# Long runs of contraction steps in the first two tiles of each phase, with later norm sums behind layer 2 and an early table load, in an eight-core streaming encoder trunk

## The chip, the cores and the metric

The kernel runs as one program on the 8 NeuronCores of one Trainium2 chip (two dies, cores 0 to 3 and 4 to 7). Each core works on its own tokens; nothing is exchanged between cores. The metric is the device time in microseconds of the slowest core. Engines are named as in the profile: PE is TensorE (PEld its weight loads), DVE is VectorE, ACT is ScalarE, POOL is GpSimd, SP is SyncE; SPq and POOLq are the queues on which DMAs are issued.

## What is computed

Four layers, all of the same outer form, on activations of width 1024 (inner width 2048):

```
h   = rms_norm(x) * (1 + scale) + shift          # scale, shift, gate from a conditioning vector
br  = h @ w_in                                   # 2, 3 or 4 branches of 2048 channels, one of them z
y   = mixer(branches)                            # 0: gated MLP over positions, 1: short conv,
                                                 # 2: conv of width 31 + layer norm, 3: pooling
x   = x + gate * ((y * silu(z)) @ w_out)         # w_out: 2048 -> 1024
```

Layer 0 applies GELU to the branches u and v, layer 2 a sigmoid to the branch ag (`glu = a * sigmoid(ag)`); a final RMS norm follows layer 3. Each core has some 2100 token columns, held in SBUF with channels on the partitions.

## The kernel before

**Groups and phases.** A core's columns are two groups, g = 0 (1074 columns with the halo, 1056 in the later layers) and g = 1 (1024 prompt columns and 32 of the decode request). Every layer runs, for g = 0 and then for g = 1, an *in phase* (`h @ w_in` and the mixer, result in `ysT`, 16 chunks of 128 channels) and an *out phase* (`ysT @ w_out`, 8 output tiles d = 0 to 7, added to x). That makes 8 in phases and 8 out phases. Below, (2,0) is layer 2, group 0.

**A tile** is 128 output channels by one group's columns, three PSUM banks wide: per contraction step (128 input channels) PE does three matmuls of 358 or 352 columns. An in tile has 8 steps (24 matmuls), an out tile 16 (48 matmuls). `tile_mm` (L456) issues them, so that nearly all matmuls of the profile have line 461. Only two such *slots* exist (`next_slot`, L282): slots take turns, and the first matmul into a slot waits until ACT or DVE has emptied it (the eviction of the tile before the last). The banks 6 and 7 beside them take norm sums and the adaLN product.

**Order of work.** `Sched` (L46) records instructions engine by engine in program order and puts a semaphore wait only where the data asks for one. Engines are in-order, so the order in the program is the order on each engine. Weights come through a ring of 8 tiles of SBUF (`pump`, L297): whenever PE is done with a tile, `release` (L315) issues the next load on the POOL queue, in a fixed order.

**Start of an in phase.** h is produced at the end of the out phase before it by DVE (`apply`, L441: `scale` L430, then `modulate` L437), 8 chunks, the last one only after the eviction of out tile 7. So the first in tile is issued in single contraction steps, each with its own wait for its chunk of h: with `fine=True` in `inproj` (L466) for layers 1 to 3. In layer 0, `inproj_first` (L477) alternates between the first two tiles at every step:

```python
for kc in range(8):
    for ci in range(2):
        tile_mm(sls[ci], nc_ // 3, [(w[:, kc, ...], hT[:, kc, ho:ho + nc_])], [wkey, "h.%d" % kc], kc == 0, kc == 7)
```

**The out phase** (`out_phase`, L502) first calls the hooks of index -1, then alternates tile 0 and tile 1 at every one of the 16 steps (L520 to L522), since the last chunks of `ysT` come late, and then goes on with tiles 2 to 7 one by one. DVE adds every tile to x (L536; for g = 1 a second, short instruction, L542, corrects the decode columns). After each tile d come the hooks of index d, which make the *other* group's next norm (`norm_hooks`, L1205):

```python
hooks = {-1: [lambda d=d: sq(d) for d in range(8)],
         1: [lambda d=d: stats(d) for d in range(8)] + [rstd],
         2: [bc]}
for d, which in ((3, (0,)), (4, (1, 2)), (5, (3, 4)), (6, (5, 6)), (7, (7,))):
    hooks[d] = [lambda i=i: apply(i) for i in which]
```

`sq` is 8 squares on ACT (L400), `stats` 24 short matmuls that sum them (L407), `rstd` is an add and a reciprocal on DVE (L413, L414) and a square root on ACT (L415, with an activation table load), `bc` a broadcast by PE into the next slot (L423) with its copy on ACT (L427).

**Layer 2** ends its in phase with a pipeline over the 16 chunks: `center` (L1007), `norm` (L1013 on DVE, then a SiLU on ACT, L1015) and `product` (L1022 on DVE).

## Time and profile before

| | |
|---|---|
| three timed runs | 2281.91, 2282.03, 2287.24 us; median 2282.03 us |
| profiled execution: span of the slowest core (core 5) | 2280.8 us |
| spans of the 8 cores in it | 2267.7 to 2280.8 us |
| mean granted PE clock, core 5 | 0.978 |
| median of die 0, of die 1 | 2272.2 us, 2274.4 us |
| PE busy on core 5 | 2135.5 us (94% of the span) |

The span runs from the first to the last instruction of one profiled execution; that execution's own time outside it is not listed, and the span lies 1.2 us below the median of the timed runs. A busy time of a group of matmuls is from the start of the first to the modelled end of the last: three matmuls alone show 0.61 us, of which some 0.15 us is the last one's way through the engine and not time that the next one must wait. So distances between starts are the better measure, and the idle time in brackets is a little low. In the waits, "PE ps L461 <- ACT ysT L649" is idle time of PE before a matmul that was ended by ACT's instruction of line 649.

### The profile page before, as it was taken

What the parts mean: (1) busy time and instruction counts of PE and PEld (TensorE: products, weight loads), DVE (VectorE), ACT (ScalarE), POOL (GpSimd) and SP (SyncE); (2) the same over time, 40 slices, a digit from 0 to 9 for tenths busy, and PEclk for the clock granted to TensorE, in tenths of its full rate; (3) what the DMA queues carried; (4) which work ended last, traced back from release to release, by engine and by line L of the source; (5) the groups of instructions that cost most, each with busy time, mean ns of one, the idle gap of its engine ahead of it and who ended that gap; (6) DMA issues with size and microseconds to landing.
All of it is one profiled execution on the core that took longest, in us unless ns stands there. A gap on an engine that the chain in (4) does not pass through costs nothing.

```text
span 2280.8 us, 41000 instructions; the slowest of 8 cores (2267.7 to 2280.8 us)
## 1 busy us (share of the span) xinstructions
PE 2135.5 (94%) x15851; PEld 1324.3 (58%) x15851; DVE 1045.9 (46%) x1482; ACT 670.2 (29%) x854; POOL 321.1 (14%) x593
## 2 busy tenths in 40 slices
PE   4999999998999999999999997999989999999996
PEld 1644655445666666666666664566655566666653
DVE  3444150442455454655545322753316566455535
ACT  3254303543011112111121334703446322303331
POOL 1012001111000100001002441104430000000000
PEclk9999999999999999999999998999999999999998
DMA  9905848057344644346445994538974444444423
GB/s 204 203 24 89 134 74 134 16 91 141 65 67 69 105 69 81 65 75 111 75 75 112 192 195 97 104 64 192 200 173 70 81 68 73 73 71 69 81 45 150
DMA packets 90637, 232.43 MB, mean 102 GB/s; under 512 B 16400, under 2 KB 41616, under 8 KB 90288
## 3 DMA queue, kind: packets, MB, share of 16 engines
q0 software_dynamic: 53264, 181.82, 45.3%
q1 hardware_dynamic: 37184, 48.00, 7.9%
q8 instruction: 130, 2.13, 0.4%
q14 instruction: 59, 0.48, 0.1%
HBM read 339.51 MB, written 9.55 MB: 153 GB/s over the span
## 4 chain that ended last, share of the span: by engine, by line
PE 82%; DVE 6%; DMA 5%; issue 2%; ACT 2%; SPq 2%; DVEq 0%; POOL 0%; ACTq 0%; POOLq 0%
PE ps L461 73%; PE ps L684 5%; DMA ring<-w_in_a 2%; SPq L130 2%; DMA ring<-w_ada 1%; PE ps L937 1%; DMA tmp<-tmp 1%; DVE tmp L893 1%; PE ps L753 1%; PE ps L749 1%; ACT hT L400 1%; DVE xb_sb L536 1%; DVE tmp L1007 1%; DMA xa_sb<-xa 0%; DVE xa_sb L536 0%
## 5 line engine op out<-in xcount | busy, mean ns | idle before, releaser
L461 PE MATMUL ps<-hT,ring 128*128 128x352 bf16 (+1 forms) x8448 | 1304.6, 316 | 30.3 <-DVE tmp L893 6.3
L461 PEld LDWEIGHTS ps<-hT,ring 128*128 128x128 bf16 x8448 | 827.8, 98 | 501.2 <-issue 50.5
L461 PE MATMUL ps<-ysT,ring 128*128 128x352 bf16 (+1 forms) x3072 | 473.6, 315 | 16.7 <-DVE xb_sb L542 4.8
L461 PEld LDWEIGHTS ps<-ysT,ring 128*128 128x128 bf16 x3072 | 298.7, 98 | 191.6 <-issue 26.2
L130 POOL DMA_DIRECT2D tmp<-tmp x256 | 128.7, 509 | 125.2 <-DVE histG L899 46.2
L684 PE MATMUL ps<-ring,hT 128*128 128x512 bf16 (+1 forms) x576 | 128.8, 383 | 4.2 <-DMA ring<-w_in_a 2.9
L893 DVE TENSOR_TENSOR tmp<-tmp,ps 128x1074 bf16<-128x1074 f32 (+3 forms) x64 | 45.5, 711 | 172.5 <-issue 97.5
L810 ACT ACTIVATE tmp<-ps 128x1074 f32<-128x1074 f32 (+1 forms) x32 | 33.9, 1058 | 261.9 <-PE ps L461 188.0
L820 DVE TENSOR_TENSOR tmp<-tmp,ps 128x1074 f32<-128x1074 f32 (+3 forms) x64 | 45.4, 710 | 140.0 <-PE ps L461 136.3
L945 ACT ACTIVATE tmp<-ps,cst_sb 128x16 bf16<-128x16 f32 (+2 forms) x160 | 69.8, 436 | 121.7 <-PE ps L937 103.4
L536 DVE SCALAR_TENSOR_TENSOR xb_sb<-ps,modT,xb_sb 128x1056 f32<-128x1056 f32 x32 | 42.1, 1317 | 128.5 <-PE ps L461 128.5
L536 DVE SCALAR_TENSOR_TENSOR xa_sb<-ps,modT,xa_sb 128x1074 f32<-128x1074 f32 (+1 forms) x32 | 42.1, 1325 | 122.8 <-PE ps L461 122.8
L684 PEld LDWEIGHTS ps<-ring,hT 128*128 128x128 bf16 (+1 forms) x576 | 55.9, 98 | 70.6 <-issue 7.6
L130 POOL DMA_DIRECT2D ring<-w_in_b x64 | 34.4, 538 | 386.0 <-PE ps L461 378.8
L837 DVE SCALAR_TENSOR_TENSOR tmp<-tmp,cst_sb 128x1074 f32<-128x1074 f32 (+1 forms) x64 | 85.1, 1329 | 7.0 <-DVE tmp L834 0.5
L841 ACT ACTIVATE ysT<-ps 128x1074 bf16<-128x1074 f32 (+1 forms) x32 | 33.9, 1058 | 184.2 <-PE ps L461 184.2
L1126 ACT ACTIVATE tmp<-ps 128x1056 f32<-128x1056 f32 (+3 forms) x64 | 39.1, 611 | 157.4 <-PE ps L461 154.5
L937 PE MATMUL ps<-tmp 128*32 128x352 bf16 (+2 forms) x2048 | 68.1, 287 | 10.5 <-DMA tmp<-tmp 8.3
L771 DVE TENSOR_TENSOR ysT<-ysT,tmp 128x1074 bf16<-128x1074 bf16 (+1 forms) x32 | 22.8, 713 | 108.0 <-ACT tmp L770 108.0
L844 DVE TENSOR_TENSOR tmp<-tmp,ps 128x1074 f32<-128x1074 f32 (+3 forms) x64 | 45.4, 709 | 55.0 <-PE ps L461 51.3
L760 DVE TENSOR_TENSOR ysT<-ps,ysT 128x512 bf16<-128x512 f32 (+2 forms) x72 | 44.1, 649 | 48.1 <-PE ps L753 47.5
L937 PEld LDWEIGHTS ps<-tmp 128*32 128x32 bf16 x2048 | 48.0, 99 | 30.7 <-issue 20.4
(156 smaller groups left out, 1667.2 us busy)
## 6 DMA issues: line engine op xcount, KB each, us to landing
ring<-w_in_b POOLq DMA_DIRECT2D x64, 512.0 KB, 5.3
ring<-w_ada POOLq DMA_DIRECT2D x48, 512.0 KB, 9.2
ring<-w_in_a POOLq DMA_DIRECT2D x48, 512.0 KB, 13.1
ring<-w_in_c POOLq DMA_DIRECT2D x48, 512.0 KB, 6.0
ring<-w_in_d POOLq DMA_DIRECT2D x32, 512.0 KB, 5.2
tmp<-tmp SPq DMA_DIRECT2D x128, 69.4 KB, 7.4
tmp<-tmp POOLq DMA_DIRECT2D x128, 69.4 KB, 6.8
tmp<-tmp SPq DMA_DIRECT2D x128, 67.5 KB, 5.7
```

The source lines that it names most:

```text
L130: h.dma_start(out=out, in_=in_, **kw).then_inc(dsm, 16)
L461: ins = h.matmul(PSB[:, 3 * sl + n, 0:W], lhsT=lw, rhs=rh[:, n * W:(n + 1) * W], start=(first and k == 0), stop=(last and k == len(pairs) ...
L536: s.op("dve", lambda h, sl=sl, xv=xv, d=d: h.scalar_tensor_tensor(out=xv, in0=PSB[:, 3 * sl:3 * sl + 3, 0:W], scalar=gate[:, 16 + d, 0:1], ...
L684: ins = h.matmul(PSB[0:n, nq, :], lhsT=hT[:, kh * 4 + kk, hc:hc + n], rhs=vw[nq * 2 + kh][:, kk, :], start=(kh == 0 and kk == 0), stop=(kh ...
L760: s.op("dve", lambda h, bank=bank, y=y: h.tensor_tensor(out=y, in0=v3(PSB[:, 4 + bank, :], 4)[:, :, 0:no], in1=y, op=ALU.mult), reads=yk, ...
L820: s.op("dve", lambda h, ps=ps, cc=cc, n=n, nb=nb, smp=smp, p=p, CG=CG: h.tensor_tensor(out=shp(p[:, H + cc + smp * H:H + cc + smp * H + n] ...
L837: s.op("dve", lambda h, p=p, a=a, c=c, wd=wd, k=k: h.scalar_tensor_tensor(out=a[:, 0:wd], in0=p[:, k:k + wd], scalar=prmT[:, c, k:k + 1], ...
L844: s.op("dve", lambda h, ps=ps, cc=cc, n=n, nb=nb, smp=smp, a=a, CG=CG: h.tensor_tensor(out=shp(tf(CG + cc, n), nb), in0=shp(a[:, cc + smp ...
L893: s.op("dve", lambda h, ps=ps, cc=cc, n=n, nb=nb, smp=smp: h.tensor_tensor(out=even_odd(G, H + cc + smp * H, n, nb), in0=pairs(tf(SIG + cc ...
L937: ins = h.matmul(PSB[32 * j:32 * j + 32, 3 * sl + bank, at:at + n], lhsT=wd[:, 4 * hf + j, b, :], rhs=R[:, 4 * hf + j, 4 * b + m0:4 * b + ...
L945: s.op("act", lambda h, hf=hf, bank=bank, at=at, o=o, k=k, d=d: h.activation(out=Y[:, hf, d:d + k], in_=PSB[:, 3 * sl + bank, at + o:at + ...
L1126: s.op("act", lambda h, ps=ps, cc=cc, n=n, nb=nb, smp=smp, pv=pv: h.activation(out=shp(pv[:, H + cc + smp * H:H + cc + smp * H + n], nb), ...
```

## The change

1. `inproj` loses `fine`, `inproj_first` goes. `inproj_pair` takes the first two tiles of an in phase in every layer: contraction steps 0 to 5 of the first tile, 0 to 5 of the second, then 6 and 7 of the first, 6 and 7 of the second.
2. The first two tiles of an out phase alternate in runs too: steps 0 to 11 of one, 0 to 11 of the other, then 12 to 15 of each; in layer 2 the cuts are at 8, 11 and 13.
3. In the two out phases of layer 2 the norm sums and `rstd` come after tile 2 instead of tile 1, `bc` after tile 3 instead of tile 2, and `apply(0)` joins 1 and 2 after tile 4.
4. After tile 4 of every out phase that has an in phase behind it, ACT runs a one-element activation with the non-trivial function that the next in phase uses first (GELU, SiLU, sigmoid, SiLU for layers 0 to 3).

```diff
-    def inproj(g, w, wkey, ci, fine=False, late=False):
+    def inproj(g, w, wkey, ci, late=False):
...
-    def inproj_first(g, w, wkey):
+    HEAD_K = 6
+
+    def inproj_pair(g, cols, late=False):
 
         sls = (next_slot(), next_slot())
-        ho, nc_ = span(g, False)
-        for kc in range(8):
-            for ci in range(2):
-                tile_mm(sls[ci], nc_ // 3, [(w[:, kc, ci * 128:(ci + 1) * 128], hT[:, kc, ho:ho + nc_])], [wkey, "h.%d" % kc], kc == 0, kc == 7)
+        ho, nc_ = span(g, late)
+        W = nc_ // 3
+        for lo, hi in ((0, HEAD_K), (HEAD_K, 8)):
+            for sl, (w, wkey, ci) in zip(sls, cols):
+                pairs = [(w[:, kc, ci * 128:(ci + 1) * 128], hT[:, kc, ho:ho + nc_]) for kc in range(8)]
+                for kc in range(lo, hi):
+                    tile_mm(sl, W, pairs[kc:kc + 1], [wkey, "h.%d" % kc], kc == 0, kc == 7)
         return sls
+
+    def warm_table(fn):
+        s.op("act", lambda h: h.activation(out=stat[:, 22:23], in_=stat[:, 20:21], func=fn), reads=["neghalf"], writes=["warm"])
...
+    CUTS = {0: (0, 12, 16), 1: (0, 12, 16), 2: (0, 8, 11, 13, 16), 3: (0, 12, 16)}
...
-        for i, e in enumerate(eorder):
+        for lo, hi in zip(CUTS[l], CUTS[l][1:]):
             for d in range(2):
-                tile_mm(first[d], W, [(ws[d][0][:, e, :], ysT[:, e, 0:nc_])], [ws[d][1], "ys.%d" % e], i == 0, i == 15)
+                for i in range(lo, hi):
+                    e = eorder[i]
+                    tile_mm(first[d], W, [(ws[d][0][:, e, :], ysT[:, e, 0:nc_])], [ws[d][1], "ys.%d" % e], i == 0, i == 15)
...
-            sls = inproj_first(g, w, wkey) if it == 0 else None
+            sls = inproj_pair(g, [(w, wkey, 0), (w, wkey, 1)]) if it == 0 else None
...
-                sc_ = inproj(g, v3(tl[0][0], 8), tl[0][1], ci, fine=(c == 0))
+                if c == 0:
+                    sc_, sh_ = inproj_pair(g, [(v3(t, 8), k, ci) for t, k in tl[:2]])
+                else:
+                    sc_ = inproj(g, v3(tl[0][0], 8), tl[0][1], ci)
                 s.op("act", lambda h, sl=sc_, CG=CG: h.activation(out=v3(tf(CG, NC), 3), in_=whole(g, sl), func=AF.Copy), writes=sk(sc_) + tk(CG, NC))
-                sh_ = inproj(g, v3(tl[1][0], 8), tl[1][1], ci)
+                if c:
+                    sh_ = inproj(g, v3(tl[1][0], 8), tl[1][1], ci)
...
+        lag = 1 if (l if g == 1 else l - 1) == 2 else 0
         hooks = {-1: [lambda d=d: sq(d) for d in range(8)],
-                 1: [lambda d=d: stats(d) for d in range(8)] + [rstd],
-                 2: [bc]}
-        for d, which in ((3, (0,)), (4, (1, 2)), (5, (3, 4)), (6, (5, 6)), (7, (7,))):
+                 1 + lag: [lambda d=d: stats(d) for d in range(8)] + [rstd],
+                 2 + lag: [bc]}
+        plan = ((4, (0, 1, 2)), (5, (3, 4)), (6, (5, 6)), (7, (7,))) if lag else ((3, (0,)), (4, (1, 2)), (5, (3, 4)), (6, (5, 6)), (7, (7,)))
+        for d, which in plan:
             hooks[d] = [lambda i=i: apply(i) for i in which]
+        if l < 4:
+            fn = (AF.Gelu, AF.Silu, AF.Sigmoid, AF.Silu)[l]
+            hooks[4] = hooks[4] + [lambda: warm_table(fn)]
```

The in phases of layers 2 and 3 are edited like that of layer 1.

## Rows read from the trace of the kernel before

**Rows 1.** The page, the costliest group: count, busy us, mean ns, idle before, releaser.

```profile
L461 PE MATMUL ps<-hT,ring 128*128 128x352 bf16 (+1 forms) x8448 | 1304.6, 316 | 30.3 <-DVE tmp L893 6.3
```

**Rows 2.** Waits of PE on core 5: us in total, times, longest us.

```profile
PE ps L407 <- ACT hT L400: 28.0, 20, 9.1
```

**Rows 3.** The chain that ended last: start us, us, what; five out tiles in one run.

```profile
1184.48 36.24 PE ps L461 x240
```

**Rows 4.** Timeline, first matmuls of out phases (0,0) and (1,1): start us, us.

```profile
270.44 0.62 PE L461 MATMUL ps<-ysT,ring 128*128 128x358 bf16 x3
...
272.02 14.41 PE L461 MATMUL ps<-ysT,ring 128*128 128x358 bf16 x93 [0.96 <-ACT tmp L770]
...
1159.55 14.15 PE L461 MATMUL ps<-ysT,ring 128*128 128x352 bf16 x93 [1.58 <-DVE tmp L844]
```

**Rows 5.** Timeline behind the first out pair: (0,0), then (0,1).

```profile
286.36 1.37 PE L407 MATMUL ps<-hT,onesD 128*32 128x352 bf16 x24
287.67 7.54 PE L461 MATMUL ps<-ysT,ring 128*128 128x358 bf16 x48
...
579.89 7.37 PE L461 MATMUL ps<-ysT,ring 128*128 128x352 bf16 x48 [0.17 <-DVE xb_sb L542]
```

**Rows 6.** Timeline of out phase (2,0), from its first matmul to the broadcast.

```profile
1461.98 0.61 PE L461 MATMUL ps<-ysT,ring 128*128 128x352 bf16 x3
...
1475.17 7.86 ACT L400 ACTIVATE hT<-xb_sb 128x1056 bf16<-128x1056 f32 x8
1475.41 0.71 DVE L1022 TENSOR_TENSOR ysT<-ysT,tmp 128x1056 bf16<-128x1056 bf16 x1 [1.09 <-ACT ysT L1015]
...
1477.62 0.48 PE L407 MATMUL ps<-hT,onesD 128*32 128x352 bf16 x6
...
1483.60 9.32 PE L461 MATMUL ps<-ysT,ring 128*128 128x352 bf16 x48
...
1492.84 0.87 PE L423 MATMUL ps<-tmp,sel 32*128 32x352 f32 x6
```

**Rows 7.** The same of out phase (2,1).

```profile
1781.72 0.71 DVE L1022 TENSOR_TENSOR ysT<-ysT,tmp 128x1056 bf16<-128x1056 bf16 x1 [1.09 <-ACT ysT L1015]
...
1789.91 9.75 PE L461 MATMUL ps<-ysT,ring 128*128 128x352 bf16 x48
...
1799.59 0.87 PE L423 MATMUL ps<-tmp,sel 32*128 32x352 f32 x6
```

**Rows 8.** Timeline, DVE in out phase (2,0): the scale of one `apply`.

```profile
1527.06 1.25 DVE L430 TENSOR_TENSOR hT<-xb_sb,tmp 128x1056 bf16<-128x1056 f32 x1
```

**Rows 9.** Stretches: length, busy (x) of PE, PEld, DVE, ACT, POOL; granted clock, DMA share, GB/s.

```profile
1477.00:1484.00 7.00, 3.87 (x31) 1.39 (x30) 2.70 (x3) 6.04 (x7) 1.07 (x2) 0.77 0.73 133
1484.00:1488.00 4.00, 4.00 (x17) 2.09 (x16) 2.71 (x2) 1.10 (x1) 0.00 (x0) 0.55 0.17 34
...
336.00:345.00 9.00, 6.88 (x47) 4.34 (x46) 1.25 (x3) 3.10 (x3) 0.54 (x1) 1.00 0.33 59
```

**Rows 10.** Timeline at the start of in phase (0,1).

```profile
333.63 0.61 PE L461 MATMUL ps<-hT,ring 128*128 128x352 bf16 x3
333.90 1.33 DVE L536 SCALAR_TENSOR_TENSOR xa_sb<-ps,modT,xa_sb 128x1074 f32<-128x1074 f32 x1 [1.59 <-PE ps L461]
...
335.38 6.87 PE L461 MATMUL ps<-hT,ring 128*128 128x352 bf16 x45 [1.14 <-DVE xa_sb L536]
...
341.89 1.28 ACT L649 ACT_TABLE_LOAD   x1 [44.66 <-PE ps L461]
...
343.19 1.99 ACT L649 ACTIVATE ysT<-ps 128x1056 bf16<-128x1056 f32 x2
344.38 5.83 PE L461 MATMUL ps<-hT,ring 128*128 128x352 bf16 x38 [2.12 <-ACT ysT L649]
```

**Rows 11.** Timeline at the start of in phase (1,0).

```profile
625.26 3.38 PE L461 MATMUL ps<-hT,ring 128*128 128x358 bf16 x21
...
629.20 11.05 PE L461 MATMUL ps<-hT,ring 128*128 128x358 bf16 x71 [0.56 <-DVE tmp L815]
```

More of the change, by code:

```diff
@@ L469, in inproj @@
         pairs = [(w[:, kc, ci * 128:(ci + 1) * 128], hT[:, kc, ho:ho + nc_]) for kc in range(8)]
-        if fine:
-            for kc in range(8):
-                tile_mm(sl, nc_ // 3, pairs[kc:kc + 1], [wkey, "h.%d" % kc], kc == 0, kc == 7)
-        else:
-            tile_mm(sl, nc_ // 3, pairs, [wkey] + ["h.%d" % kc for kc in range(8)])
-        return sl
-    def inproj_first(g, w, wkey):
+        tile_mm(sl, nc_ // 3, pairs, [wkey] + ["h.%d" % kc for kc in range(8)])
+        return sl
+    HEAD_K = 6
+    def inproj_pair(g, cols, late=False):
         sls = (next_slot(), next_slot())
-        ho, nc_ = span(g, False)
-        for kc in range(8):
-            for ci in range(2):
-                tile_mm(sls[ci], nc_ // 3, [(w[:, kc, ci * 128:(ci + 1) * 128], hT[:, kc, ho:ho + nc_])], [wkey, "h.%d" % kc], kc == 0, kc == 7)
-        return sls
+        ho, nc_ = span(g, late)
[5 more added lines that the diff above has]
+                    tile_mm(sl, W, pairs[kc:kc + 1], [wkey, "h.%d" % kc], kc == 0, kc == 7)
+        return sls
+    def warm_table(fn):
+        s.op("act", lambda h: h.activation(out=stat[:, 22:23], in_=stat[:, 20:21], func=fn), reads=["neghalf"], writes=["warm"])
     def whole(g, sl, late=False):
@@ L883, in front @@
             ci = c % 2
-            sg = inproj(g, v3(tl[1][0], 8), tl[1][1], ci, fine=(c == 0))
+            if c == 0:
+                sg, sa = inproj_pair(g, [(v3(tl[b][0], 8), tl[b][1], ci) for b in (1, 0)])
+            else:
+                sg = inproj(g, v3(tl[1][0], 8), tl[1][1], ci)
             s.op("act", lambda h: h.activation(out=v3(tf(SIG, NI), 3), in_=whole(g, sg), func=AF.Sigmoid), writes=sk(sg) + tk(SIG, NI))
-            sa = inproj(g, v3(tl[0][0], 8), tl[0][1], ci)
+            if c:
+                sa = inproj(g, v3(tl[0][0], 8), tl[0][1], ci)
             G = tb(GB[ci], GW)
@@ L1116, in in_phase3 @@
                 tl = [get(sp) for sp in specs]
-            sp_ = inproj(g, v3(tl[0][0], 8), tl[0][1], c % 2, fine=(j == 0), late=True)
+            if j == 0:
+                sp_, sz_ = inproj_pair(g, [(v3(t, 8), k, c % 2) for t, k in tl], True)
+            else:
+                sp_ = inproj(g, v3(tl[0][0], 8), tl[0][1], c % 2, late=True)
             po = PV[j % 3]
@@ L1127, in in_phase3 @@
                     out=shp(pv[:, H + cc + smp * H:H + cc + smp * H + n], nb), in_=ps, func=AF.Copy), writes=sk(sp_) + pk)
-            sz_ = inproj(g, v3(tl[1][0], 8), tl[1][1], c % 2, late=True)
+            if j:
+                sz_ = inproj(g, v3(tl[1][0], 8), tl[1][1], c % 2, late=True)
             s.op("act", lambda h, sl=sz_, c=c: h.activation(out=v3(ysT[:, c, 0:NC], 3), in_=whole(g, sl, True), func=AF.Silu), writes=sk(sz_) + ["ys.%d" % c])
```

## The prediction, made before the changed kernel was run

> **What bounds the kernel now.** The page comes first: of the span of 2280.8 us PE is busy for 94%, and the costliest group is its matmuls of L461 [rows 1]. The matmuls of L461 with `hT` have only 30.3 us of idle time before 8448 of them. So nothing large stands still; the question is which short gaps of PE the change closes. The list of what PE waited for is the second view [rows 2]: its head, 28.0 us in 20 waits of the norm sums (L407) for ACT's squares (L400), is mostly where the sums sit behind layer 2. The third view is the chain, for the pace without gaps [rows 3]: 240 matmuls in 36.24 us are 0.151 us each at 352 columns, and by the columns 0.154 us at 358. A gap is then the distance between two starts less the matmuls in it. The last view is the timeline at the 16 phase starts, with the granted clock of a few stretches.
>
> **First pair of an out phase, its start.** PE begins tile 0 with three matmuls at 270.44 and then stands before the first step of tile 1 until 272.02, because that slot is still being evicted [rows 4]. Three matmuls cost 0.46 us, so 1.12 us are lost, the 0.96 us in brackets plus 0.16 us of modelled tail. The six out phases of layers 0, 1 and 3 show 0.96, 0.84, 1.07, 1.58, 1.12 and 1.12 us (the first and the largest in [rows 4]); with six tails, 7.65 us. With the change tile 0 has 36 matmuls first, 5.5 us of cover, three times the longest gap, and its own slot was free at the old start too. I take the whole **7.65 us**; the bounds are 6.7 (no tails) and 7.7. The chunks of `ysT` are no cost: the last four steps come as late as before, within 1.4 us, and step 11 of tile 0 is needed after 5 us, when in layers 0, 1 and 3 only the chunks put last are still in work.
>
> **The same pair, its end.** Tile 2 needs tile 0's slot. Now the norm sums (L407, 1.30 us) lie in between and hide the eviction: no idle time in (0,0), 0.17 us in (0,1), where L542 follows [rows 5]. The runs let tile 0 end 12 matmuls before tile 1 instead of 3, so the three cases with g = 1 give **0.5 us**; those with g = 0 give nothing.
>
> **Layer 2, out phase (2,0).** The eight squares queue on ACT behind the last SiLU and run from 1475.17 to 1483.03; the sums are ready to start at 1477.62, follow them one by one, and tile 2 starts at 1483.60 [rows 6]. Unhindered sums take 1.30 us [rows 5], so 4.7 us are lost. Tile 2 then lasts until the broadcast at 1492.84, 9.24 us for 48 matmuls where 7.25 us are normal [rows 3, 6]: the granted clock is 0.77 in the stretch of the waits and 0.55, which is almost all at the lower level of 1.2 GHz, in the 4 us behind it [rows 9]. That is 2.0 us more. With the lag: the pair starts at 1461.98 and runs without the first gap, but chunk 15 is ready only at 1476.12 [rows 6], about 1476.3 with the signal. Behind it lie step 15 of tile 0 and steps 13 to 15 of tile 1, 12 matmuls or 1.8 us: pair done at 1478.1, tile 0 at 1476.8. An eviction begins 0.27 us after the next tile has started on PE (333.63 to 333.90) and takes 1.33 us [rows 10], so tile 2 starts at 1478.5 and ends at 1485.7; by then the squares are long done, the sums take 1.3 us, and we are at 1487.0, where before 1492.84 stood: **5.8 us**. The first gap of this phase is no separate gain, since chunk 15 holds the pair.
>
> **Out phase (2,1)** the same way: chunk 15 ends at 1782.43 [rows 7], pair done at 1784.4, tile 0 at 1783.1; eviction, L542 (as in [rows 5] 0.2 to 0.3 us) and signals put tile 2 at 1785.1, its end at 1792.3, the sums at 1793.6, against 1799.59 now [rows 7]: **5.9 us**. What is late next: add, reciprocal and square root have one tile's time between the sums and the broadcast, as now, when in (0,0) it is enough behind two evictions [rows 5]; after the change only one eviction stands before them, so the broadcast does not wait. Three `apply` after tile 4 instead of two: each is a scale of 1.25 us [rows 8] and a modulation that I bound by as much, so 7.5 us with 1.3 us of eviction, 1.6 us over a tile's 7.25; the next two hooks need 6.3 us each and take it back before h is wanted. Should they not, the next in phase starts up to 1 us late. The slot turns are unchanged in number, so the 1.3 us before the tile behind the broadcast stays.
>
> **In phase (0,1).** PE starts at 333.63, does three matmuls, and waits with the second tile's first step for the eviction of out tile 7, until 335.38; then, at the pair's end near 342.1, for a GELU that has a table load of 1.28 us (341.89) before it, until 344.38 [rows 10]. After: 18 matmuls (2.7 us) cover the eviction, which ends at 335.23; 48 matmuls end at 340.85, tile 0 six matmuls earlier at 339.95; signal, GELU of 1.05 us and signal free its slot at 341.4. Against 344.38: **3.0 us**. The same one-element activation stands in the kernel once already, and the first GELU of (0,0) has no load before it, so I count the load as gone; it moves to where ACT is idle for over 40 us [rows 10]. I count its delay as 1.30 us, 341.89 to 343.19. The Trainium skill (ScalarE: Activation LUTs, What ACT_TABLE_LOAD costs) puts a switch of table at about 2.66 us, since a drain of 1.38 us comes on top of the load; by that this term would be 1.4 us larger, and the row disagrees, since the activation begins 0.02 us after the load.
>
> **The other in phases.** In (1,0) tile 0 stops before chunk 7: 21 matmuls from 625.26 end at 628.5, the rest starts at 629.20 [rows 11], 0.7 us. In the new order chunk 7 is needed only after 39 matmuls, at 631.3, so that gap goes. But now both tiles end close together: the pair at 632.65, tile 0 at 631.7, and ACT needs 0.25 + 1.07 us (the 1.05 us of the GELU, by the columns) and a signal, so the third tile starts at 633.2; now it starts at 629.20 + 27 matmuls = 633.35. So 0.7 us of waiting for h becomes 0.5 us of waiting for ACT, and **0.2 us** are left. Worked the same way, (1,1), (2,0), (2,1) and (3,0) give 0.3, 0.2, 0.4 and 0.2 us, and (3,1) loses 0.2 us, since for g = 1 layer 3 empties its first tile in three copies, an estimated half longer than one; (0,0) stands under saturated weight loads and counts as nothing. Together **1.0 us**, between -1 and 2. In (2,0) and (2,1) the early sigmoid is what keeps this from being a loss of 1.3 us each.
>
> **Sum.** 7.65 + 0.5 + 5.8 + 5.9 + 3.0 + 1.0 = 23.9 us. Against the profiled span, 2280.8 - 23.9 = 2256.9 us; the median of the runs lies 1.2 us above that span, so I forecast **2258.0 us**. The POOL queue issues the weight loads in the same order, each behind the same tile's last matmul; no DMA is added.
>
> **Rivals.**
> - *The clock is not won back.* The pair in layer 2 now waits itself, for chunk 15 and then for the slot (some 1.7 and 0.4 us). If that lets the clock fall as 6 us of loose sums do now, 2.0 and 2.4 us are kept: 24 - 4.4 gives 2262.4 us. Against it: in (0,1) PE stands 2.1 us and the clock stays at 1.00 [rows 9, 10].
> - *The gain is taken back downstream*, by a weight load or a DVE pipeline that does not move with PE. The candidate is layer 0, where DMAs are densest: without the first 1.1 and the 3.0 us, 2262.1 us. Against it: the loads are issued by PE's own releases, so they move along.
> - *The change doesn't do what it says*: the early table is not the one needed. Then (0,1) keeps 1.3 us and (2,0) and (2,1) lose 1.3 us each, together 3.9 us: 2261.9 us. Against it: the kernel's own early GELU works.
> - *The short stops at the pairs' ends cost the clock* (the side of slower). Every in phase now has a stop of about 0.5 us right behind its pair, and the two slots cycle without slack there. If such a stop brings the lower clock of [rows 9] for some 4 us, 2.2 us per phase start, 16 of them make 35 us; with the 4.4 us of layer 2 not won, 2282.0 - 19.5 + 35.2 = 2297.7 us. It decides from 9 of the 16 starts on. Against it: longer stops before the first GELU leave the clock at 1.00 [rows 9, 10]. The Trainium skill (TensorE: Matmul & The Clock Gate, A second HAM failure mode: psum-queue depth-cycling) describes this mechanism, short idle spells between groups of matmuls that cycle through PSUM banks and make the clock swing; the trace does not agree for stops up to 2.1 us.
>
> **How the numbers follow.** The forecast case has 0.79; the clock not won back 0.09, taken back downstream 0.06, a wrong table 0.03, the clock lost at the pairs 0.02, and 0.01 for something that leaves no change. A measurement of this kernel can tell about 0.3%, 6.8 us, from no change; all cases but the last two lie well beyond it: faster 0.97, within 0.01, slower 0.02. The range takes the bounds of the terms (7.65 by -1, layer 2 by 1 each way per phase, the small in phases by -2 to +1) and the three cases near 2262: 2253.5 to 2264.5 us.
>
> **What would show it.** Right: the x3 rows before a gap vanish at the six out starts; L407 behind layer 2 runs its 24 matmuls in about 1.4 us, with tile 2 before it and no stretch at a clock of 0.55; the waits of L407 for L400 fall from 28 us to some 19; no ACT_TABLE_LOAD before the first L649, L841, L885 and L1129 of a phase, but one in the out phase; waits of about 0.5 us for ACT at every in phase's third tile. Wrong: such a wait of over 1 us, tile 3 of layer 2 or its broadcast waiting for the square root, or a lower granted clock at phase starts.

## The result and the profile after

The changed kernel takes 2260.09 us (median of four runs, 2257.95 to 2261.17), the kernel before beside it 2281.91 to 2287.24; the ratio is 0.9892, with a 95% interval of 0.9880 to 0.9903. That is 1.08%, or 24.7 us less, where 23.9 were forecast, and a predicted time of 2258.0 us with a range of 2253.5 to 2264.5. The difference of the two medians is smaller, 21.9 us (2282.03 - 2260.09): the slowest core scatters by some us from run to run. In a second measurement on another chip the ratio was 0.9901 (0.9883 to 0.9919), with medians of 2282.95 and 2260.80 us, 22.2 us apart. Some executions show one die or both at a lower granted clock and take longer (2402.64 us for one of the kernel before); they are left out of every ratio and median here, and where only such a profile exists, the cores of its undisturbed die are read.

The first view of the page after: the span of the slowest core, and the two groups of L461.

```profile
span 2257.8 us, 41011 instructions; the slowest of 8 cores (2246.2 to 2257.8 us)
...
L461 PE MATMUL ps<-hT,ring 128*128 128x352 bf16 (+1 forms) x8448 | 1299.7, 315 | 26.0 <-DVE ysT L768 5.5
...
L461 PE MATMUL ps<-ysT,ring 128*128 128x352 bf16 (+1 forms) x3072 | 468.9, 313 | 10.9 <-DVE xb_sb L550 5.1
```

The first of the two answers to [rows 1]: 4 us less idle time only. The second group had 473.6 us busy and 16.7 us idle before. Most of the gain is in out phases and in how fast matmuls ran: both groups are also busy for less time, by 4.9 and 4.7 us, with the same counts. The waits of PE after (total us, times, longest):

```profile
PE ps L407 <- ACT hT L400: 22.1, 9, 8.9
...
PE ps L461 <- ACT ysT L657: 0.8, 2, 0.4
```

L407 waited 28.0 us in 20 cases [rows 2] and now 22.1 in 9; what is left lies before the first layer (20.1 us) and behind the last (2.0 us). The lines that answer to [rows 6], out phase (2,0), are these (core 4; L1038 is the product, L544 the addition to x):

```profile
1451.52 12.33 PE L461 MATMUL ps<-ysT,ring 128*128 128x352 bf16 x81
...
1464.03 0.61 PE L461 MATMUL ps<-ysT,ring 128*128 128x352 bf16 x3 [0.18 <-DVE ysT L1038]
1464.73 7.87 ACT L400 ACTIVATE hT<-xb_sb 128x1056 bf16<-128x1056 f32 x8
1464.96 0.71 DVE L1038 TENSOR_TENSOR ysT<-ysT,tmp 128x1056 bf16<-128x1056 bf16 x1 [1.08 <-ACT ysT L1031]
1465.82 1.97 PE L461 MATMUL ps<-ysT,ring 128*128 128x352 bf16 x12 [1.18 <-DVE ysT L1038]
...
1468.01 7.38 PE L461 MATMUL ps<-ysT,ring 128*128 128x352 bf16 x48 [0.22 <-DVE xa_sb L544]
1475.32 1.38 PE L407 MATMUL ps<-hT,onesD 128*32 128x352 bf16 x24
...
1476.62 7.39 PE L461 MATMUL ps<-ysT,ring 128*128 128x352 bf16 x48
...
1483.94 0.87 PE L423 MATMUL ps<-tmp,sel 32*128 32x352 f32 x6
```

The pair runs 81 matmuls without a gap, waits for chunks 14 and 15, has the 12 matmuls behind chunk 15, and tile 2 follows after 0.22 us of idle time. Tile 2 takes 7.31 us, start to start, instead of 9.24, and the sums 1.30 instead of 6. The granted clock there (the last figures of a stretch are clock, DMA share, GB/s):

```profile
1463.00:1470.00 7.00, 5.42 (x35) 3.00 (x34) 4.23 (x5) 6.80 (x8) 1.08 (x2) 1.00 0.25 35
1470.00:1480.00 10.00, 10.00 (x83) 6.23 (x82) 4.19 (x3) 2.67 (x4) 0.54 (x1) 1.00 0.70 124
```

The start of in phase (0,1), which answers to [rows 10], has one stop left, before the third tile: 7.72 us from the phase's first matmul to 342.43, of which 48 matmuls are 7.25, so 0.47 us; and no table load; the load stands at 298.32, in the out phase, when ACT has nothing else to do. All seven in phases behind an out phase are like that: before, each had a load ahead of its first non-trivial function, now each has it in the out phase before.

```profile
298.32 1.28 ACT L488 ACT_TABLE_LOAD   x1
...
334.71 7.32 PE L461 MATMUL ps<-hT,ring 128*128 128x352 bf16 x48
...
341.23 1.99 ACT L657 ACTIVATE ysT<-ps 128x1056 bf16<-128x1056 f32 x2 [41.41 <-PE ps L461]
...
342.43 3.74 PE L461 MATMUL ps<-hT,ring 128*128 128x352 bf16 x24 [0.40 <-ACT ysT L657]
```

**The phases one by one.** For each core of each profiled execution I took the start of the first matmul on `ysT` or `hT` of a phase from the timeline, and from the starts the lengths (the last one up to the last matmul). Medians of the 8 cores in us, in brackets largest less smallest (not given everywhere); the kernels with other names are the experiments below.

```
phase       before       changed      cuts only    pairs only   lag only     no lag       cut at 4     bc mid
out(0,0)    63.2 (0.0)   62.1 (0.0)   62.1         63.2         63.2         62.1         62.1         61.2
out(0,1)    62.5 (0.0)   61.2 (0.0)   61.2         62.5         62.5         61.2         61.2         60.1
out(1,0)    63.3 (0.0)   62.1 (0.0)   62.1         63.3         63.3         62.1         62.1         61.2
out(1,1)    63.2 (0.0)   61.2 (0.0)   61.2         63.2         63.2         61.2         61.2         60.1
out(2,0)    68.7 (0.4)   62.9 (0.0)   68.7         68.7         63.3         68.8         62.9         62.1
out(2,1)    68.9 (0.2)   63.2 (0.0)   69.0         69.0         64.0         68.9         63.2         62.1
out(3,0)    62.1 (0.0)   60.9 (0.0)   60.9         62.1         62.1         60.9         60.9         60.0
out(3,1)    70.3 (0.2)   68.8 (0.0)   68.8         70.3         70.3         68.8         68.8         67.6
in(1,0)     237.5 (0.0)  237.5 (0.0)  237.5        237.5        237.6        237.5        237.1        237.5
in(1,1)     231.3 (0.0)  231.4 (0.0)  231.3        231.1        231.3        231.4        230.5        231.4
in(3,0)     146.5 (0.0)  146.4 (0.0)  146.5        146.4        146.5        146.4        146.0        146.4
in(3,1)     146.8 (0.0)  147.1 (0.0)  146.7        147.1        146.7        147.1        146.2        147.1
in(0,0)     216.7 (5.1)  215.9 (7.5)  216.7 (5.6)  216.5 (3.2)  217.1 (4.5)  215.4 (7.1)  216.6 (5.2)  216.5 (6.9)
in(0,1)     226.1 (5.7)  221.3 (3.8)  225.5 (5.3)  221.5 (6.7)  225.1 (11.1) 220.7 (4.8)  219.7 (5.4)  219.9 (6.1)
in(2,0)     241.2 (4.0)  241.8 (3.5)  241.7 (1.8)  244.5 (7.4)  240.8 (2.8)  241.6 (5.0)  242.2 (4.4)  241.7 (7.0)
in(2,1)     236.7 (7.1)  237.1 (7.6)  236.6 (4.3)  238.3 (13.8) 233.8 (4.0)  235.2 (6.8)  234.5 (4.0)  237.9 (6.9)
```

Twelve of the sixteen phases repeat to 0.1 us over the eight cores and over kernels in which they are built alike; there, terms of half a microsecond can be read. The exceptions among the twelve are out(2,0) and out(2,1) where the sums stand behind tile 1 (0.2 to 2.5 us between cores) and out(3,1), 0.2 us. The four others differ by 2 to 14 us between the cores of one execution. The time of the whole kernel is that of the unluckiest core, so it carries this scatter; the spans of all cores do less. Their mean over all fast executions is 2274.5 us for the kernel before and 2252.3 us for the changed one (second measurement): 22.2 us.

### The profile page after: what moved, and what is told of

It reads as the page before. It is cut to its first block, busy times and chain, and to the rows that moved or that the text cites. A ratio compares the mean times of both kernels' runs of the same rounds, so it can differ in the third digit from the quotient of the medians.

```text
span 2257.8 us, 41011 instructions; the slowest of 8 cores (2246.2 to 2257.8 us)
## 1 busy us (share of the span) xinstructions
PE 2122.4 (94%) x15851; PEld 1320.6 (58%) x15851; DVE 1046.8 (46%) x1482; ACT 672.8 (30%) x861; POOL 322.3 (14%) x593
## 4 chain that ended last, share of the span: by engine, by line
PE 83%; DMA 6%; DVE 5%; issue 2%; ACT 2%; SPq 1%; POOL 1%; DVEq 0%; ACTq 0%; POOLq 0%
PE ps L461 73%; PE ps L692 5%; DMA tmp<-tmp 2%; DMA ring<-w_in_a 1%; SPq L130 1%; DMA ring<-w_ada 1%; DVE tmp L909 1%; PE ps L953 1%; PE ps L761 1%; PE ps L757 1%; DVE tmp L1023 1%; DMA xa_sb<-xa 0%; PE ps L407 0%; DMA ysT<-tmp 0%; DVE ysT L1038 0%
## 5 line engine op out<-in xcount | busy, mean ns | idle before, releaser
L461 PE MATMUL ps<-hT,ring 128*128 128x352 bf16 (+1 forms) x8448 | 1299.7, 315 | 26.0 <-DVE ysT L768 5.5
L461 PEld LDWEIGHTS ps<-hT,ring 128*128 128x128 bf16 x8448 | 826.0, 98 | 493.3 <-issue 45.5
L461 PE MATMUL ps<-ysT,ring 128*128 128x352 bf16 (+1 forms) x3072 | 468.9, 313 | 10.9 <-DVE xb_sb L550 5.1
L461 PEld LDWEIGHTS ps<-ysT,ring 128*128 128x128 bf16 x3072 | 297.3, 97 | 182.3 <-issue 19.2
L821 ACT ACTIVATE tmp<-ps 128x1074 f32<-128x1074 f32 (+1 forms) x32 | 33.9, 1059 | 265.3 <-PE ps L461 191.3
L544 DVE SCALAR_TENSOR_TENSOR xb_sb<-ps,modT,xb_sb 128x1056 f32<-128x1056 f32 x32 | 42.2, 1318 | 120.7 <-PE ps L461 120.2
L544 DVE SCALAR_TENSOR_TENSOR xa_sb<-ps,modT,xa_sb 128x1074 f32<-128x1074 f32 (+1 forms) x32 | 42.5, 1328 | 116.9 <-PE ps L461 116.8
L853 ACT ACTIVATE ysT<-ps 128x1074 bf16<-128x1074 f32 (+1 forms) x32 | 33.9, 1059 | 192.5 <-PE ps L461 192.5
L900 ACT ACTIVATE tmp<-ps 128x1074 f32<-128x1074 f32 (+1 forms) x32 | 33.9, 1059 | 143.4 <-PE ps L461 107.5
L779 DVE TENSOR_TENSOR ysT<-ysT,tmp 128x1074 bf16<-128x1074 bf16 (+1 forms) x32 | 22.8, 714 | 107.9 <-ACT tmp L778 107.9
L657 ACT ACTIVATE ysT<-ps 128x1074 bf16<-128x1074 f32 (+1 forms) x32 | 33.7, 1059 | 126.6 <-PE ps L461 126.6
```

The costliest lines, as they stand in the source:

```text
L461: ins = h.matmul(PSB[:, 3 * sl + n, 0:W], lhsT=lw, rhs=rh[:, n * W:(n + 1) * W], start=(first and k == 0), stop=(last and k == len(pairs) ...
L544: s.op("dve", lambda h, sl=sl, xv=xv, d=d: h.scalar_tensor_tensor(out=xv, in0=PSB[:, 3 * sl:3 * sl + 3, 0:W], scalar=gate[:, 16 + d, 0:1], ...
L821: s.op("act", lambda h, sl=sc_, CG=CG: h.activation(out=v3(tf(CG, NC), 3), in_=whole(g, sl), func=AF.Copy), writes=sk(sc_) + tk(CG, NC))
```

## The experiments

**One part of the change on the kernel before: the runs in the out phases.**

```diff
-        for i, e in enumerate(eorder):
-            for d in range(2):
-                tile_mm(first[d], W, ...)
+        for lo, hi in zip(CUTS[l], CUTS[l][1:]):
+            for d in range(2):
+                for i in range(lo, hi):
+                    tile_mm(first[d], W, ...)
```

> The kernel before with only the runs of 12 and 4 steps (8, 3, 2, 3 in layer 2) in the first pair of the out phases. My sum gives 7.65 us at the six starts of layers 0, 1 and 3 and 0.5 us at the pairs' ends: 8.1 us, ratio 0.996. In layer 2 nothing is won: the pair still waits for chunk 15 and the sums for the squares, so L407 keeps its 28 us of waits. Rival, the gain is taken back downstream: the three matmuls in front of a gap vanish from the timeline all the same, but the ratio stays above 0.998.

Measured: ratio 0.9968 (0.9954 to 0.9981), 7.3 us. The six out phases of layers 0, 1 and 3 got 1.1, 1.3, 1.2, 2.0, 1.2 and 1.5 us shorter, 8.3 us; layer 2 kept its 68.7 and 69.0 us, and L407 its 28.0 us. Gap by gap the sum holds too: 1.12, 1.17, 1.23, 1.91, 1.28 and 1.45 us were to be won, and the unrounded lengths give 1.09, 1.23, 1.21, 1.94, 1.28 and 1.50. At the start of (0,0) the three matmuls before the gap are one run now:

```profile
271.93 14.90 PE L461 MATMUL ps<-ysT,ring 128*128 128x358 bf16 x96
286.76 1.37 PE L407 MATMUL ps<-hT,onesD 128*32 128x352 bf16 x24
```

**The pairs alone**, on the kernel before: `inproj_pair` as in the change, with no early table load, the old alternation in out phases and the old hooks.

> The kernel before with only the pairs at the starts of the in phases, without the early table load, the out runs and the later sums. My terms: 3.0 us in (0,1) less 1.3 us, since the GELU's table load stays on PE's path; 1.0 us in the other seven less 1.3 us each in (2,0) and (2,1), where the sigmoid's load now lies on the path. Together 0.1 us: no change, within 1.5 us either way. Rival, that waits for h are worth their full 0.7 us in six phases: 4 to 6 us faster, ratio 0.998.

Measured: ratio 1.0009 (0.9980 to 1.0038), no change, as the sum said; the interval does not quite exclude the rival's 4 us. The trace does: of the 0.7 us of waiting for h in (1,0) nothing is left in the length of the phase, 237.5 us as before, (1,1) gains 0.2, (3,0) 0.1, and (3,1) loses 0.3. In (0,1) the third tile starts 1.74 us earlier (9.00 us after the phase's start for 10.74), for 1.7 us expected; that this phase is 4.6 us shorter is taken up below, with the clock. The sigmoid's load is where it was expected, between the pair and the third tile of (2,0), on core 1:

```profile
1213.40 7.52 PE L461 MATMUL ps<-hT,ring 128*128 128x358 bf16 x48
1220.19 1.28 ACT L898 ACT_TABLE_LOAD   x1 [42.79 <-PE ps L461]
1221.49 1.07 ACT L898 ACTIVATE tmp<-ps 128x1074 f32<-128x1074 f32 x1
1222.70 9.51 PE L461 MATMUL ps<-hT,ring 128*128 128x358 bf16 x61 [1.78 <-ACT tmp L898]
```

**The later sums alone**, on the kernel before:

```diff
+        lag = 1 if (l if g == 1 else l - 1) == 2 else 0
-                 1: [lambda d=d: stats(d) for d in range(8)] + [rstd],
-                 2: [bc]}
+                 1 + lag: [lambda d=d: stats(d) for d in range(8)] + [rstd],
+                 2 + lag: [bc]}
```

> The kernel before with only the sums of layer 2 moved behind tile 2. By my sum nearly all of the 11.7 us of layer 2 come from this move alone: 11 to 11.7 us faster, ratio 0.995, and the granted clock stays at 1.00 behind the pair. If the clock does not come back, 7 us, ratio 0.997.

Measured: ratio 0.9963 (0.9950 to 0.9976), 8.4 us; the two phases 5.4 and 4.9 us shorter, 10.3 of the 11 to 11.7 expected. The clock came back: tile 2 takes 7.31 us, start to start. What is missing is mostly the runs' share, since with alternation at every step tile 0 ends 3 matmuls before tile 1 and tile 2 waits longer for its slot, 1.13 us in brackets instead of 0.22:

```profile
1481.43 7.37 PE L461 MATMUL ps<-ysT,ring 128*128 128x352 bf16 x48 [1.13 <-DVE xa_sb L536]
1488.74 1.37 PE L407 MATMUL ps<-hT,onesD 128*32 128x352 bf16 x24
```

So of 11.4 us in layer 2 (5.75 and 5.68), 10.3 come from the lag alone and 1.1 only from lag and runs together; the runs alone win nothing there.

**Is the slow tile behind the sums a matter of PE standing?** The kernel before, with matmuls put into the waits:

```diff
+        def fill():                       # six matmuls 128x256 into bank 7, not read by anyone
+            ...
+        def stats_fill(d):
+            stats(d)
+            if hot and d < 7:             # hot: the two out phases of layer 2
+                fill()
-                 1: [lambda d=d: stats(d) for d in range(8)] + [rstd],
+                 1: [lambda d=d: stats_fill(d) for d in range(8)] + [rstd],
```

> The kernel before with six matmuls of 256 columns into an unused bank behind each of the first seven norm sums of layer 2's two out phases; nothing is moved, their result is not used. If the low clock behind those sums comes from PE standing, the fillers keep it at 1.00 and tile 2 takes 7.3 us again instead of 9.3 and 9.7: about 4 us faster than before, ratio 0.998, while the 5.6 to 6 us of the sums stay. If the clock falls for another reason (data, the squares' or the DMAs' activity), tile 2 keeps its 9.3 us and the time is that of before or up to 1 us more.

Measured: ratio 0.9983 (0.9942 to 1.0023). The mechanism is as expected and the price is not: the clock stays at 1.00 in both stretches where it was 0.77 and 0.55 [rows 9],

```profile
1475.00:1484.00 9.00, 9.00 (x78) 5.21 (x77) 3.06 (x3) 6.20 (x7) 1.08 (x2) 1.00 0.64 118
1484.00:1488.00 4.00, 4.00 (x29) 2.57 (x27) 2.35 (x1) 1.50 (x2) 0.00 (x0) 1.00 0.00 0
```

and tile 2 takes 7.32 us,

```profile
1482.16 0.83 PE L1213 MATMUL ps<-sc 128*128 128x256 bf16 x6
1482.92 0.33 PE L407 MATMUL ps<-hT,onesD 128*32 128x352 bf16 x3
1483.18 7.39 PE L461 MATMUL ps<-ysT,ring 128*128 128x352 bf16 x48
1490.50 0.87 PE L423 MATMUL ps<-tmp,sel 32*128 32x352 f32 x6
```

but the phases are only 0.6 and 0.5 us shorter (68.1 and 68.4 us). The ratio of 0.998 that was expected came out within an interval of 9 us to either side; by the phases 1.1 us were won and not 4. A step of sum and filler takes 1.02 us, a square 0.97, so the fillers set the pace of the sums: these last 7.4 us from 1475.78 on instead of 6.0. What the clock gave, the fillers took. The expectation had counted them as free. Still, the question is answered: the clock fell because PE did little, not because of the squares, which are all still there, or of the transfers, which are nearly as dense as before in the stretch of the sums (DMA share 0.64 for 0.73).

**Undoing single parts of the change.** First the early table load:

```diff
-        if l < 4:
-            fn = (AF.Gelu, AF.Silu, AF.Sigmoid, AF.Silu)[l]
-            hooks[4] = hooks[4] + [lambda: warm_table(fn)]
```

> The changed kernel without the early table load. By my sum the load comes back onto PE's path where the first tile of a pair needs a new table: 1.3 us in in phase (0,1), where the stop of PE before the third tile grows from 0.73 to about 2.0 us, and 1.3 us each in (2,0) and (2,1); layers 1 and 3 begin with a copy and hide the load as before. Together 3.9 us slower than the changed kernel. Rival, the load is hidden by something else or costs its drain as well: (0,1) unchanged, or 2.7 us longer.

Measured: ratio to the kernel before 0.9908 (0.9879 to 0.9937), against 0.9892 and 0.9901 with the load: the 1.6 to 3.7 us lie inside the interval. The stop before the third tile is, on core 0,

```profile
339.81 1.99 ACT L657 ACTIVATE ysT<-ps 128x1056 bf16<-128x1056 f32 x2
341.00 5.23 PE L461 MATMUL ps<-hT,ring 128*128 128x352 bf16 x34 [1.67 <-ACT ysT L657]
...
1221.77 8.44 PE L461 MATMUL ps<-hT,ring 128*128 128x358 bf16 x54 [1.78 <-ACT tmp L900]
```

1.67 us of idle time in (0,1) where the changed kernel has 0.40, and 1.78 in (2,0) where it has 0.50: 1.27 and 1.28 us, the load's length and nothing on top. In (2,1) the third tile starts 9.11 us after the phase's start instead of 7.83, 1.28 us again, so the three together are the 3.9 us expected. One thing goes the other way: in (1,1) the third tile starts at 7.83 us without the early load and at 8.10 us with it, and the phase is 0.3 us shorter (231.1 for 231.4). The copy of its first tile starts later there when the load came early; why stays open.

Then the lag, with `lag = 0`:

> The changed kernel with the sums of layer 2 back behind tile 1. By my sum out phases (2,0) and (2,1) lose 5.8 and 5.7 us: they last 68.7 and 68.9 us again, of which 2.0 and 2.4 us are tile 2 at the lower clock. With the pair ending a little later than before (chunk 15 and 12 matmuls behind it) the sums wait a little less, so 0.3 us less may be lost. If the moves of layer 2 were not what won there, the two phases stay under 64 us.

Measured: ratio 0.9940 (0.9911 to 0.9968), 9 to 11 us lost. The two phases last 68.8 and 68.9 us, and the row of tile 2 is back at 9.7 us (core 5):

```profile
1470.70 0.48 PE L407 MATMUL ps<-hT,onesD 128*32 128x352 bf16 x3 [0.49 <-ACT hT L400]
1471.11 9.73 PE L461 MATMUL ps<-ysT,ring 128*128 128x352 bf16 x48
```

Then layer 2's own cuts, with `2: (0, 12, 16)`:

> The changed kernel with the cut of layers 0, 1 and 3 (12 and 4 steps) in layer 2 too. Chunk 15 is then followed by one step of tile 0 and four of tile 1, 15 matmuls instead of 12, so each of the two out phases of layer 2 lasts 0.45 us longer; the first tile is done as early, so the eviction is better hidden and 0.2 us of that may come back. If the finer cuts matter because chunks 8 to 11 come late, it is 1 us or more per phase.

Measured: ratio 0.9891 (0.9857 to 0.9925); the two phases last 63.0 and 63.2 us, against 62.9 and 63.2. Neither 0.45 us nor 1 us: the finer cuts are worth 0.1 us at most. The three more matmuls behind chunk 15 and the better hidden eviction cancel out: behind chunk 15 the 15 matmuls of the pair and the 48 of tile 2 run as one row of 63, without the stop of 0.22 us.

**Looking for more: the broadcast.** In every out phase the tile behind the broadcast (L423) waits for the eviction of the tile just before it, since the broadcast has taken the other slot. First try: banks 6 and 7 for it, two thirds after tile 2, the last third in the middle of tile 3.

```diff
-                 2 + lag: [bc]}
+                 2 + lag: [lambda: bc.part((0, 1))],
+                 ("mid", 3 + lag): [lambda: bc.part((2,))]}
```

> The changed kernel with the broadcast of the norm factor in banks 6 and 7 instead of a slot: two thirds of it where it was, the last third in the middle of the next out tile. The two slots then take turns over the eight out tiles, and no tile waits for the eviction of the one just before it. Every one of the eight out phases has that wait now, 0.8 us (g = 0) or 1.1 us (g = 1) of idle time in brackets: the out phases get 0.8 to 1.3 us shorter each, together 8 us, ratio to the kernel before 0.986. Rival: the next wait takes its place, the last third comes too late for apply, or the other parity of the slots costs as much at the start of the next in phase; then out phases shrink and in phases grow, and the sum stays.

Measured: ratio 0.9879 (0.9844 to 0.9913), and the out phases are as long as in the changed kernel for g = 0 (62.1, 62.1, 63.0, 60.9 us) and 0.3 us shorter for g = 1. The wait is gone and another cost has come:

```profile
293.59 0.86 PE L433 MATMUL ps<-tmp,sel 32*128 32x352 f32 x4
...
294.38 3.86 PE L475 MATMUL ps<-ysT,ring 128*128 128x358 bf16 x24
...
298.17 0.85 PE L433 MATMUL ps<-tmp,sel 32*128 32x352 f32 x2
298.96 13.22 PE L475 MATMUL ps<-ysT,ring 128*128 128x358 bf16 x85
```

Four of these fp32 matmuls take 0.79 us, start to start, and two take 0.79 us as well; all six together show 0.87 us [rows 6]. The three parts of the broadcast stand in different 32-row strips of the array. That they run beside each other is the reading that fits; in any case a broadcast costs the same whole or in part, and cutting it in two doubles it.

Second try, undivided, in the middle of tile 3, into the slot that tile 4 will use:

```diff
-        def bc():
-            sl = next_slot()
+        def bc(peek=False):
+            sl = rr["i"] ^ 1 if peek else next_slot()
...
-                 2 + lag: [bc]}
+                 ("mid", 3 + lag): [lambda: bc(True)]}
```

The other edits were measured beside it: the pairs cut behind step 4 (`HEAD_K = 4`), both together, and the changed kernel once more.

> The changed kernel unaltered, as the measure for the three beside it on the same chip: ratio to the kernel before 0.989, as first measured, within 0.002.

> The changed kernel with the in phases' pairs cut behind step 4 instead of 6. The first tile then ends 12 matmuls, 1.8 us, before the second, which covers signal, copy and signal (1.5 us): the stop before the third tile (0.7 us in (0,1), some 0.75 in the others, start to start) goes. Chunk 7 of h is wanted 5.1 us after the start, 1.3 us after it is there. 0.6 to 0.75 us in each of the seven in phases behind an out phase, about 0.9 in (3,1), 0 in (0,0): 4 to 5 us faster than the changed kernel. Rival: as in the kernel with the pairs alone, what is won at the third tile is lost again before the phase ends, because a stage of DVE or of the DMAs sets the pace there; then in(1,0), in(1,1), in(3,0) and in(3,1), which repeat to 0.1 us, stay as they are.

> The changed kernel with the whole broadcast (six matmuls, one group of some 0.8 us) put into the middle of the out tile behind it, into the slot that the next tile will use. Split in two groups it cost 0.79 us twice and won nothing; undivided it costs 0.8 us once, its slot was evicted 2 us before, and its copy has the second half of the tile, 3.6 us, to finish. What goes is the wait for the eviction of the tile just before, start to start 1.64 - 0.8 = 0.8 us for g = 0 and 1.1 us for g = 1 in each of the eight out phases: about 7.5 us faster than the changed kernel, every out phase shorter by 0.7 to 1.1 us, no in phase longer. Rival: another wait takes its place, above all apply coming half a tile later; then out phases shrink and in phases start with a wait for h.

> Both of the last two edits together. They close different gaps, so their gains add: 11 to 12 us faster than the changed kernel, ratio to the kernel before 0.984. If they use the same slack of DVE before h is ready, less than the better of the two more is won.

Measured, ratios to the kernel before: the changed kernel 0.9901 (0.9883 to 0.9919), cut at 4 0.9863 (0.9846 to 0.9881), broadcast in the middle 0.9862 (0.9840 to 0.9883), both 0.9851 (0.9835 to 0.9868), with medians of 2260.80, 2253.49, 2252.71 and 2250.66 us. The broadcast shortens the eight out phases by 0.9, 1.1, 0.9, 1.1, 0.8, 1.1, 0.9 and 1.2 us, 8.0 us for 7.5 expected; no steady in phase changes, so the rival falls. At (0,0) only one distance of 0.80 us is left where 1.66 us were:

```profile
285.72 11.23 PE L461 MATMUL ps<-ysT,ring 128*128 128x358 bf16 x72
...
296.88 0.87 PE L423 MATMUL ps<-tmp,sel 32*128 32x352 f32 x6
297.68 14.60 PE L461 MATMUL ps<-ysT,ring 128*128 128x358 bf16 x94
```

The cut at 4 takes 0.4, 0.9, 0.4 and 0.9 us from the four steady in phases, and the stop in (0,1) is gone, the first 89 matmuls running as one:

```profile
331.87 13.44 PE L461 MATMUL ps<-hT,ring 128*128 128x352 bf16 x89
```

By the lengths of the steady phases that is 2.6 us. The start of the third tile can be read in the others as well, and comes 0.56 us earlier in (0,1), 0.41 in (2,0) and 0.67 in (2,1): 4.2 us in all, within the 4 to 5 us expected. The stop of 0.63 us in (1,0) gives only 0.4 because another gap opened: the first run is now 12 matmuls, 1.8 us, and the eviction of the other slot with its correction (L550) lasts until 618.90, so the 13th matmul starts 0.40 us behind the 12th instead of 0.154. The same stands in (2,0) and (3,0), where the correction follows too. With both edits the phases show both effects unchanged (61.3, 60.1, 62.1 us and so on, in(1,1) 230.5), 10.6 us in the steady twelve; the whole kernel moves by 10.1 us by the medians, from 2260.80 to 2250.66, and by 11.4 us by the ratios. This version is faster than the kernel before and than the changed one, whose interval (0.9883 to 0.9919) lies above its own.

## Why the prediction was right

Point by point, in us:

```
step of the prediction                         forecast   measured
starts of the six pairs, layers 0, 1, 3        7.65       } 8.3 (lengths of the six out phases)
their ends, g = 1                              0.5        }
layer 2, out phase (2,0)                       5.8        5.8
layer 2, out phase (2,1)                       5.9        5.7
in phase (0,1), stops at its start             3.0        3.0 (10.75 - 7.72)
in phase (0,1), clock behind the stops         nothing    1.7 on six of the eight cores
the other in phases                            1.0        0.0 up to the third tile; -0.3 in the four steady lengths
```

**The starts and ends of the pairs** are right within 0.2 us. The kernel with the cuts alone isolates them: same phases, same lengths, no interplay with the rest.

**Layer 2** is right in amount and in its parts: the forecast put the end of the sums 25.0 us behind the pair's start, and in the trace it is 25.1 (1476.62 - 1451.52). The waits of the sums and the low clock behind them are one cause with two effects: the sums stood between two long tiles while PE did little, and the tile behind paid. The kernel with fillers separates them, the lag removes both. The clock rival falls: the pair now has stops of its own, 0.18, 1.18 and 0.22 us in brackets, and the clock stays at 1.00 on all eight cores. One part of my working was generous to the lag: 1.1 of the 11.4 us need the runs, since tile 2 now stands directly behind the pair. And one reading was wrong: the 28.0 us of [rows 2] are not mostly layer 2. On core 5 19.8 us of them lie before the first layer, 2.0 behind the last and only 6.2 in the two out phases of layer 2, so they could not fall to some 19 us; they fell by 6, to 22.1. The sum didn't use this number.

**In phase (0,1)** is right: from its first matmul to its third tile 7.72 us instead of 10.75. Of that, 1.27 us are the early table load, as the kernel without it shows; the Trainium skill's 2.66 us for a switch of table (ScalarE: Activation LUTs, What ACT_TABLE_LOAD costs) are not confirmed here, the row says 1.28 us with an activation 0.02 us behind.

**What the prediction overlooked there.** It read on core 5 that PE stands 2.1 us in (0,1) and the clock stays at 1.00, and used this against two of its rivals. In the same execution six of the eight cores show something else. Core 3, then core 5:

```profile
341.23 8.95 PE L461 MATMUL ps<-hT,ring 128*128 128x352 bf16 x48 [2.12 <-ACT ysT L649]
341.00:346.00 5.00, 4.77 (x22) 2.69 (x23) 0.00 (x0) 1.03 (x2) 0.00 (x0) 0.66 0.56 104
...
344.38 7.32 PE L461 MATMUL ps<-hT,ring 128*128 128x352 bf16 x48 [2.12 <-ACT ysT L649]
344.00:349.00 5.00, 4.62 (x31) 3.06 (x32) 0.00 (x0) 1.96 (x3) 0.00 (x0) 1.00 0.60 108
```

Behind the two stops of 1.14 and 2.12 us the granted clock falls to the lower level for a while on core 3, and from the third tile to the fifth PE needs 9.9 us there and 8.24 us on core 5. That is so on 22 of 32 cores over the four profiled kernels with the old start of (0,1): six in the kernel before, four with the cuts only, six with the lag only, six with the fillers. It is so on none in the kernels with the new start, also where one stop of 1.7 us is left (the pairs alone, and the four cores read without the early load). So `inproj_pair` won another 1.7 us on most cores that no term had: in(0,1) is 4.8 us shorter in the median, and 3.0 and 1.7 make 4.7. That both stops are needed for it was not tested by itself.

**The other in phases** are the term that was mis-sized. The forecast said 0.2 to 0.4 us each, and -0.2 in (3,1), because a wait for h of 0.7 us turns into a wait for ACT of 0.5 us. Measured, start of the phase to its third tile, the changed kernel needs 8.02 us in (1,0) for 8.08, 8.10 in (1,1) for 8.00, 8.02 in (2,0) for 8.08, 7.83 in (2,1) for 7.98, 7.83 in (3,0) for 7.94, and 8.30 in (3,1) for 7.98, where the wait for ACT is 0.98 us. The six add up to nothing. The rows of (1,0):

```profile
617.93 7.52 PE L461 MATMUL ps<-hT,ring 128*128 128x358 bf16 x48
...
624.74 1.07 ACT L821 ACTIVATE tmp<-ps 128x1074 f32<-128x1074 f32 x1 [41.18 <-PE ps L461]
...
625.95 1.23 PE L461 MATMUL ps<-hT,ring 128*128 128x358 bf16 x7 [0.50 <-ACT tmp L821]
```

The copy starts 0.34 us behind the tile's last matmul (617.93 + 42 x 0.154 = 624.40), not 0.25, and the stop is 0.63 us, not 0.5. That took most of each 0.2 us; in (1,1) 0.27 us more are the price of the early load, as the kernel without it shows.

**The sum** was helped by luck. The terms as measured are 8.3 + 5.8 + 5.7 + 3.0 = 22.8 us, and 1.25 us in the mean over the cores for the clock in (0,1): 24.0 us, against the 23.9 us forecast, because the 1.0 us that failed to come and the 1.25 us that had no term nearly cancel. The whole kernel shows 24.7 us by the ratio, 21.9 and 22.2 us by the medians and 22.2 us by the mean of all cores; these differ by more than the two misses, so the time of the whole kernel can't tell them apart, and only the phases can.

**The rivals.** Nothing was taken back downstream: in(0,1), the candidate, is 4.8 us shorter in the median, not longer. The stops at the pairs' ends did not cost the clock: they are 0.4 to 1.0 us, and in the changed kernel no core falls to the lower level in the first 30 us of any phase from out(0,0) on. The premise that spoke against both clock rivals, longer stops at a clock of 1.00, holds on two cores of eight only; they fell all the same, with shorter stops. The early table is the one needed: no load stands before the first non-trivial function of any in phase any more. The Trainium skill (TensorE: Matmul & The Clock Gate, A second HAM failure mode: psum-queue depth-cycling) describes short idle spells between groups of matmuls that cycle through PSUM banks and make the clock swing. The trace agrees for the two stops at the old start of (0,1), 1.14 and 2.12 us, on six cores of eight, against what the prediction says of it; it shows no such case for the single stops of 0.2 to 1.2 us in the changed kernel's pairs. What brought the lower clock in layer 2, on all eight cores, were 6 us in which eight short sums came one by one.

## What to carry to other kernels

When two accumulators alternate, order the steps by what ends the wait: a long first run on the slot that is free covers the eviction of the other, and a last run on the second one covers the eviction of the first, so the length of the last run should exceed signal, copy and signal, here 1.5 us or 10 matmuls, which 6 did not and 12 did. The first run is bounded in the same way: 18 matmuls covered the other slot's eviction, and 12 left 0.25 us where a correction follows it. Small work that waits for another engine should not sit between two long tiles; one tile later it costs only its own 1.3 us, and the clock that it would have cost comes back as well. A reading of the clock on one core is not yet one of the kernel: look at all eight. Where phases differ in scatter, read each edit in the phases that repeat to 0.1 us and leave the whole time to the final comparison.

## What the runs showed of the hardware

- Groups of six, four and two fp32 matmuls, on three, two and one 32-row strips, showed 0.87, 0.86 and 0.85 us of busy time, with 0.79 to 0.80 us to the next tile's start: splitting such a group doubles its cost.
- A stretch in which PE did sums of 0.33 us every 0.97 us brought the granted clock to 0.77 and then 0.55; with 0.83 us of filler in each interval it stayed at 1.00, though the squares were the same and the DMA share was 0.64 for 0.73.
- Two stops of PE of 1.14 and 2.12 us at the old start of phase (0,1) were followed by the lower clock on 22 of 32 cores (0.66 over 5 us on core 3 of the kernel before), at a price of 1.7 us; one stop of 1.7 us on none of 12.
- ACT's copy of a tile began 0.34 us after the time at which the tile's last matmul was through by the pace of 0.154 us, and PE resumed 0.14 us after the copy, in phase (1,0). By the same reckoning ACT began 0.18 us behind the tile in (0,1) and 0.56 in (1,1), so the hand-over from PE to ACT and back cost 0.3 to 0.7 us beside the copy itself.
